# Taking the reciprocal deviation out of the up projection's operand

## What is computed

```python
mod = (silu(c) @ w_ada + b_ada)            # sh1, sc1, g1, sh2, sc2, g2
x = layer_norm(ALPHA * x + g1 * (merged @ w_o), ln1_g, ln1_b)
h2 = x * (1 + sc2) + sh2
up, gt = split(h2 @ w_up, 2)
f = (silu(gt) * up) @ w_down
x = layer_norm(ALPHA * x + g2 * f, ln2_g, ln2_b)
```

## Time and profile before

| what | value |
|---|---|
| median of 3 runs | 526.11 us (525.12 to 526.12) |
| the profiled execution's own time | 526.49 us |
| its span | 524.9 us |
| TensorE busy | 505.6 us, 96% of the span |
| VectorE busy | 294.0 us, 56% |
| ScalarE busy | 223.4 us, 43% |
| GpSimd busy | 90.6 us, 17% |
| mean granted TensorE clock | 0.99 of full speed |

### The profile page before, as it was taken

The page is one execution under the profiler, slowest core; times in us unless marked ns, Lnnn a source line. Parts: engine busy times, 40 slices in busy tenths (PEclk is TensorE's granted clock), DMA queues, the critical chain, the costliest instruction groups (busy, mean ns, idle before and its releaser), DMA issues.

```text
span 524.9 us, 10079 instructions
## 1 busy us (share of the span) xinstructions
PE 505.6 (96%) x3932; PEld 462.0 (88%) x3932; DVE 294.0 (56%) x568; ACT 223.4 (43%) x370; POOL 90.6 (17%) x133
## 2 busy tenths in 40 slices
PE   5899999999999999998999799998999999999997
PEld 3678879888778998997998499998999999999996
DVE  0556676858445453446975966543644445466344
ACT  1434533325435553447436454563444444333312
POOL 2000211126900000000350509631011100000000
PEclk9899999999999999989999999999999999999999
DMA  8999997495996820842654716599777754354102
GB/s 258 394 393 392 381 393 263 143 379 195 326 333 195 272 82 11 253 145 80 240 183 141 240 58 188 165 372 321 277 259 259 261 164 168 136 210 161 41 0 91
DMA packets 85437, 115.80 MB, mean 221 GB/s; under 512 B 3785, under 2 KB 67465, under 8 KB 84884
## 3 DMA queue, kind: packets, MB, share of 16 engines
q1 hardware_dynamic: 83572, 102.76, 58.0%
q0 software_dynamic: 1824, 12.47, 6.4%
HBM read 111.94 MB, written 13.57 MB: 239 GB/s over the span
## 4 chain that ended last, share of the span: by engine, by line
PE 81%; DMA 9%; SPq 3%; DVE 3%; ACT 2%; issue 1%; POOL 0%; DVEq 0%; POOLq 0%; ACTq 0%
PE psum L750 22%; PE psum L752 21%; PE psum L751 21%; DMA raw<-in_w_in 4%; DMA ada_s<-in_w_ada 2%; PE psum L923 2%; PE psum L1043 2%; DMA x_tok<-in_x_sample 2%; PE psum L996 1%; PE psum L1029 1%; PE psum L987 1%; PE psum L782 1%; PE psum L1227 1%; DMA k_early<-in_cache_kv_b 1%; PE psum L771 1%
## 5 line engine op out<-in xcount | busy, mean ns | idle before, releaser
L750 PE MATMUL psum<-act_hi,w_hi 128*128 128x288 f32 x736 | 222.9, 303 | 6.6 <-DVE act_lo L1873 3.3
L499 DVE TENSOR_TENSOR w_lo<-raw,w_hi 128x1024 fp32r<-128x1024 f32 (+1 forms) x120 | 146.0, 1220 | 148.1 <-ACT w_hi L494 147.9
L751 PE MATMUL psum<-act_lo,w_hi 128*128 128x288 f32 x736 | 218.4, 297 | 0.0
L752 PE MATMUL psum<-act_hi,w_lo 128*128 128x288 f32 x736 | 218.0, 296 | 0.0
L494 ACT ACTIVATE w_hi<-raw 128x1024 fp32r<-128x1024 f32 (+1 forms) x120 | 124.1, 1040 | 101.4 <-PE psum L752 81.6
L750 PEld LDWEIGHTS psum<-act_hi,w_hi 128*128 128x128 f32 x736 | 139.4, 189 | 19.7 <-issue 12.5
L752 PEld LDWEIGHTS psum<-act_hi,w_lo 128*128 128x128 f32 x736 | 139.8, 190 | 0.0
L751 PEld LDWEIGHTS psum<-act_lo,w_hi 128*128 128x128 f32 x736 | 139.6, 190 | 0.1
L750 PE MATMUL psum<-f_hi,w_hi 128*128 128x288 f32 x176 | 52.3, 297 | 0.0
L751 PE MATMUL psum<-f_lo,w_hi 128*128 128x288 f32 x176 | 51.9, 295 | 0.0
L752 PE MATMUL psum<-f_hi,w_lo 128*128 128x288 f32 x176 | 51.8, 294 | 0.0
(11 more groups left out here) (214 smaller groups left out, 588.1 us busy)
## 6 DMA issues: line engine op xcount, KB each, us to landing
ada_s<-in_w_ada SPq DMA_DIRECT2D x22, 1024.0 KB, 10.2
raw<-in_w_up SPq DMA_DIRECT2D x22, 1024.0 KB, 5.4
raw<-in_w_in SPq DMA_DIRECT2D x17, 1024.0 KB, 9.8
raw<-in_w_down SPq DMA_DIRECT2D x10, 1024.0 KB, 5.1
out<-in_cache_kv_a POOLq DMA_DIRECT2D x16, 504.0 KB, 6.8
raw<-in_w_o SPq DMA_DIRECT2D x4, 1024.0 KB, 5.8
raw<-in_w_in SPq DMA_DIRECT2D x4, 768.0 KB, 11.0
kvin<-in_cache_kv_a SPq DMA_DIRECT2D x8, 256.0 KB, 3.5
```

Source lines behind the costliest of these rows:

```text
L499: nc.vector.tensor_tensor(part(w_lo, slot4, by_rows), raw_half(rslot, hh, by_rows), part(w_hi, slot4, by_rows).bitcast(F32), ALU.subtract) ...
L750: nc.tensor.matmul(out, hi_l, hi_r, start=start, stop=False, skip_group_check=True)
L751: nc.tensor.matmul(out, hi_l, lo_r, start=False, stop=False, skip_group_check=True)
L752: return nc.tensor.matmul(out, lo_l, hi_r, start=False, stop=stop, skip_group_check=True)
```

## The change

The operand of the up projection becomes h2 * std = (x - mean) * scale + bias * std. The factor 1/std is applied after the matmuls: to each gate unit ahead of the silu, and to each silu ahead of the product. The reciprocal, still in place in `rstd`, moves behind the last `h2_rest`.

- ScalarE scales tiles by the channel scale into `h2_t`: tiles 0 to 3, not yet centred, behind the square of tile 6 and ahead of the next `w_hi`. Tiles 4 to 7, centred by GpSimd, follow between its `act_hi` instructions. `act_hi` becomes a plain copy.
- VectorE makes for tiles 0 to 3 mean * scale - `h2_t` (`minus_centred`), and for every tile std * bias -/+ `h2_t` (`h2_shifted`). `centre_pair` is gone.
- GpSimd makes the sample tokens from `xT`, std and the conditioning, and centres `xT` tiles 0 to 3 too.
- TensorE transposes the two conditioning rows ahead of tile 5 of the first three units.
- In all 11 pairs VectorE has four instructions more, two `gate_t` and two scalings of `silu_t`. TensorE's waits on `silu_ready` become waits on `gate_scaled`.

```diff
         ada_ring(pe, ADA2 + 1)
-        ada_turn(pe, 10)
-        ada_turn(pe, 11)
...
             for k in range(KT):
+                if k == 5:
+                    ada_turn(pe, 10)
+                    ada_turn(pe, 11)
...
                 elif q < 2:
                     pe.wait_ge(f_ready, j * 2 + (q - 1))
                 else:
-                    pe.wait_ge(silu_ready, j * 2 + (q - 1))
+                    pe.wait_ge(gate_scaled, j * 2 + (q - 1))
...
+            if m == 6:
+                for k in range(4):
+                    nc.scalar.activation(h2_t[:, k, 0:PROMPT], xT[:, k, 0:PROMPT], ACT.Copy, scale=mod[:, 32 + k, 0:1]).then_inc(weighted, 1)
             if 4 <= m < 7:
                 hi_static(act, H_UP + m - 4)
...
         h2_leading(1)
+        h2_weighted(4)
         h2_leading(2)
+        h2_weighted(5)
         h2_sample_leading(2, 2, KT)
-        for m in range(3, KT):
+        h2_leading(3)
+        h2_weighted(6)
+        h2_weighted(7)
+        for m in range(4, KT):
             h2_leading(m)
...
                 if q < 2:
-                    act.wait_ge(half_used, nb + 1)
+                    act.wait_ge(gate_scaled, j * 2 + (q + 1))
...
-                    nc.scalar.activation(silu_t[:, q, :], psum[:, q, 0:TOK], ACT.Silu).then_inc(silu_ready, 1)
+                    nc.scalar.activation(silu_t[:, q, :], gate_t[:, q, :], ACT.Silu).then_inc(silu_ready, 1)
...
         dve.wait_ge(off_ready, 2)
-        centre_pair(0)
+        minus_centred(0)
+        minus_centred(1)
         dve.wait_ge(std_ready, 1)
-        V.reciprocal(rstd[:], rstd[:]).then_inc(rstd_ready, 1)
...
+        h2_shifted(0)
+        h2_shifted(1)
         h2_rest(0)
         h2_sample_rest(2, 0, 2)
         h2_rest(1)
-        centre_pair(2)
-        dve.wait_ge(dve_link.sem, dve_link.n)
-        h2_scaled(2)
-        h2_scaled(3)
+        minus_centred(2)
+        minus_centred(3)
+        h2_shifted(2)
+        h2_shifted(3)
         h2_rest(2)
         h2_sample_rest(5, 2, KT)
...
+                if q < 2:
+                    dve.wait_ge(half_used, nb + 1)
+                    if not isinstance(j, int) or j >= 1:
+                        dve.wait_ge(silu_ready, j * 2 + (q - 1))
+                    V.tensor_tensor(gate_t[:, q, :], psum[:, q, 0:TOK], rstd[:], ALU.mult).then_inc(gate_scaled, 1)
                 if q >= 2:
+                    dve.wait_ge(silu_ready, fi + 1)
+                    V.tensor_tensor(silu_t[:, q - 2, :], silu_t[:, q - 2, :], rstd[:], ALU.mult).then_inc(silu_scaled, 1)
+                    dve.wait_ge(silu_scaled, fi + 1)
...
+        pool.wait_ge(centred_s, 1)
+        h2_sample(0, 2)
         centre(4)
-        pool.wait_ge(centred_s, 1)
-        pool.wait_ge(rstd_ready, 1)
-        h2_sample(0, 2)
         h2_sample(2, KT)
         centre(6)
-        pool.wait_ge(centred, 2)
+        pool.wait_ge(weighted, 4)
+        pool.wait_ge(less_mean, 4)
+        centre(0)
+        centre(2)
```

More of the change, by code:

```diff
@@ L361, in build @@
     part_sum, _ = sb("part_sum", [128, 2, TOK], F32, o_tmp + 7 * TOK * 4)
-    off_mean, _ = sb("off_mean", [128, TOK], F32, o_tmp + TOK * 4)
+    off_mean, _ = sb("off_mean", [128, TOK], F32, o_tmp + 11 * TOK * 4)
+    bias_s, _ = sb("bias_s", [128, KT, SAMPLE], F32, o_tmp + 12 * TOK * 4)
+    gate_t, _ = sb("gate_t", [128, 2, TOK], F32, o_tmp + 9 * TOK * 4)
+    assert 12 * TOK + KT * SAMPLE <= 3840
     off_sq, _ = sb("off_sq", [128, TOK], F32, o_tmp + 2 * TOK * 4)
@@ L415, in build @@
         "sums_done", "off_ready", "var_ready", "std_ready", "rstd_ready"))
-    centred = sem("centred")
+    centred, less_mean, weighted = sem("centred"), sem("less_mean"), sem("weighted")
+    gate_scaled, silu_scaled = sem("gate_scaled"), sem("silu_scaled")
     quarters_done, quarters_x, quarters_sq = sem("quarters_done"), sem("quarters_x"), sem("quarters_sq")
@@ L1477, in h2_leading, with h2_weighted @@
             act.wait_ge(h2_ready, m + 1)
-            nc.scalar.activation(act_hi[:, m, 0:PROMPT], h2_t[:, m, 0:PROMPT], ACT.Identity,
-                                 bias=mod[:, 24 + m, 0:1]).then_inc(h2_hi, 1)
+            nc.scalar.activation(act_hi[:, m, 0:PROMPT], h2_t[:, m, 0:PROMPT], ACT.Copy).then_inc(h2_hi, 1)
+        def h2_weighted(m):
+            act.wait_ge(centred, m // 2 - 1)
+            nc.scalar.activation(h2_t[:, m, 0:PROMPT], xT[:, m, 0:PROMPT], ACT.Copy, scale=mod[:, 32 + m, 0:1]).then_inc(weighted, 1)
         def h2_sample_leading(part_n, k0, k1):
@@ L1877, in h2_rest @@
             dve.wait_ge(h2_hi, H2_HI_AT[m])
-            V.scalar_tensor_tensor(act_lo[:, m, 0:PROMPT], h2_t[:, m, 0:PROMPT], mod[:, 24 + m, 0:1], act_hi[:, m, 0:PROMPT].bitcast(F32),
-                                   ALU.add, ALU.subtract).then_inc(h2_lo, 1)
-        h2_scaled(0)
-        h2_scaled(1)
+            V.tensor_tensor(act_lo[:, m, 0:PROMPT], h2_t[:, m, 0:PROMPT], act_hi[:, m, 0:PROMPT].bitcast(F32),
+                            ALU.subtract).then_inc(h2_lo, 1)
+        h2_shifted(0)
+        h2_shifted(1)
         h2_rest(0)
@@ L1892, in _ @@
         for m in range(4, KT):
-            if m in (4, 6):
-                dve.wait_ge(centred, m // 2 - 1)
-            h2_scaled(m)
+            h2_shifted(m)
             h2_rest(m - 1)
         h2_rest(KT - 1)
+        dve.wait_ge(h2_ready, KT)
+        dve.wait_ge(h2s_ready, 2)
+        V.reciprocal(rstd[:], rstd[:]).then_inc(rstd_ready, 1)
         ada_add(10)
@@ L2059, in h2_sample @@
             by_batch = lambda i: mod[:, 8 * i + k0:8 * i + k1, 1:9].unsqueeze(3).broadcast_to([128, nk, DEC_B, DEC_T])
-            step(nc.gpsimd.tensor_tensor(hs, xT[:, k0:k1, PROMPT:TOK], by_token, ALU.mult))
-            step(nc.gpsimd.tensor_tensor(hs4, hs4, by_batch(4), ALU.mult))
-            nc.gpsimd.tensor_tensor(hs4, hs4, by_batch(3), ALU.add).then_inc(h2s_ready, 1)
+            bs = bias_s[:, k0:k1, :]
+            xs4 = xT[:, k0:k1, PROMPT:TOK].rearrange("p k (b t) -> p k b t", t=DEC_T)
+            nc.gpsimd.tensor_tensor(hs4, xs4, by_batch(4), ALU.mult).then_inc(pool_step, 1)
+            pool.wait_ge(std_ready, 1)
+            nc.gpsimd.tensor_tensor(bs.rearrange("p k (b t) -> p k b t", t=DEC_T),
+                                    by_token.rearrange("p k (b t) -> p k b t", t=DEC_T), by_batch(3), ALU.mult).then_inc(pool_step, 1)
+            steps.n = steps.n + 2
+            pool.wait_ge(pool_step, steps.n)
+            nc.gpsimd.tensor_tensor(hs, hs, bs, ALU.add).then_inc(h2s_ready, 1)
+        pool.wait_ge(centred_s, 1)
+        h2_sample(0, 2)
         centre(4)
-        pool.wait_ge(centred_s, 1)
-        pool.wait_ge(rstd_ready, 1)
-        h2_sample(0, 2)
         h2_sample(2, KT)
         centre(6)
-        pool.wait_ge(centred, 2)
+        pool.wait_ge(weighted, 4)
+        pool.wait_ge(less_mean, 4)
+        centre(0)
+        centre(2)
+        pool.wait_ge(centred, 4)
+        pool.wait_ge(rstd_ready, 1)
         pool.wait_ge(h2_lo, KT + 2)
```

23 lines of the change are left out of this document (13 added, 10 removed).

## The result

The changed kernel takes 539.46 us (median of 4 runs, 535.24 to 541.43) against 525.83 (525.12 to 526.12) in the same comparison. The two medians are 13.6 us apart, 2.6%. The ratio estimated over the runs is 1.022, 95% interval [1.017, 1.0274], so slower is clear, and that it is over 2% is not. Slower was forecast, but by 5.5 us, and 539.46 is outside the range. The profiled execution took 538.55 us, its span is 536.9 (12.0 more), the mean granted clock 0.98.

What follows compares the result with a forecast made beforehand. TensorE, busy 505.6 of 524.9 us, was taken as the bound. Terms 1.6 + 0.9 + 0 + 3.0 + 0 = +5.5 gave 532.0 profiled, 531.6 us as median; range 526.0 to 536.0, the forecast's own 529.5 to 534.

Steps and rivals of the forecast that it cites:

- Step 7: Late w_up load near 365: loads and cache copies shift together, 0; bounds -1.5 and +1.5.
- Rival D: Slower by more: clock falls already in the conditioning matmuls or twice (+1.75), late load grows (+1.5): 534.9; 8%.
- Step 5: Clock at the gap before tile 2: falls as before at the same 1.75, so 0; bounds -1.75 and +1.75.
- Step 3: Third operand tile starts +1.6 later, with three GpSimd centrings holding VectorE up by 2.6; contains steps 1 and 2.
- Step 1: Layer norm statistics come +1.2 later, as four ScalarE weightings stand ahead of the next w_hi.
- step 2: First operand tile starts +0.2 later, at about 295.2; ScalarE's second row copy is what is late.
- step 4: Transposes moved ahead of tile 5 lose their cover in TensorE's gap: +0.9, between 0.7 and 1.4.
- step 6: First two pairs of the up projection queue behind VectorE and stall TensorE: +3.0, bounds 1.15 and 4.

Runs made afterwards that it cites:

- e8: Changed kernel with weightings behind the partial sums, GpSimd's centrings of tiles 0 to 3 after the last act_lo, first pair's gate scalings first, copies later and spaced: 524.44 us.
- e11: e8 with both transposes back ahead of the first tile and GpSimd's scalings of xT after the second pair's products: 523.31 us.
- e5: Changed kernel without GpSimd's copies of the sample caches to the outputs: 531.97 us.
- e6: Kernel before the change, without GpSimd's copies of the sample caches to the outputs: 525.09 us.
- e12: Kernel before the change, with GpSimd's burst of nine cache copies begun later and the later copies moved by two units: 529.88 us.
- e2: Changed kernel with the old pairs, so the factor 1/std is left out of gate and silu: 530.87 us.
- e7: Changed kernel with both gate scalings of the first pair ahead of the first w_lo on VectorE: 534.5 us.
- e1: Kernel before the change, with the change's pairs alone and the old layer norm: 533.65 us.
- e4: Changed kernel with GpSimd's centring of tiles 0 to 3 moved behind its wait for VectorE's last act_lo of the samples: 534.14 us.
- e3: Changed kernel with ScalarE's four weightings of tiles 0 to 3 moved behind the copy of the partial sums: 535.69 us.
- e10: Changed kernel with only the cache copies begun later and spaced at 4 units, all outputs written: 531.5 us.
- e9: Kernel before the change, with only the cache copies begun later and spaced at 4 units: 524.64 us.

## Why the prediction was wrong

The 12.0 us between the two profiled executions split as below. The first two rows are read from the two traces. The other four rest on the kernels named in the last column. The 13.6 us between the medians can't be split in this way.

| step | predicted | measured | from |
|---|---|---|---|
| ahead of the change | 0 | +0.30 | square of tile 6, 282.79 against 282.49 |
| 1 to 3, third tile | +1.6 | +2.07 | 301.75 - 282.79 = 18.96 against 16.89 |
| 4, transposes | +0.9 | +0.86 | third tile to first gate, 7.60 in e8, 6.74 in e11 (304.32 - 297.58) |
| 5, clock | 0 | +1.18 | third tile to first gate, 10.23 - 7.60 after, 8.19 - 6.74 before |
| 6, first pairs | +3.0 | +3.07 | B of e5 less B of e6, 218.60 - 215.53 |
| 7, late load | 0 | +4.52 | B less that of the kernel without copies, 6.32 after, 1.80 before |

**Step 7 failed**, the one I gave a sentence: put at 0, it measured +4.52. "Loads and cache copies all hang on the same chain and shift with it": the fifth load shifted by 7.5 us (339.8 to 347.3), the burst only by 5.15. GpSimd's own chain starts 7.7 later (the scalings of `xT`, 321.56 against 313.83), but it has a wait in it that isn't on TensorE's: GpSimd waited 4.40 us for `gain_raw` before, and 2.09 after. Why that wait got shorter no run shows. The runs fall in line by how far behind the burst's start the load that TensorE waits for is issued, and in e12 only the burst was moved:

| kernel | load issued behind the burst's start, us | load takes, us | TensorE idles, us |
|---|---|---|---|
| e2 (new stage, old pairs) | 6.8 | 16.7 | 0.85 |
| before | 6.7 | 17.4 | 1.53 |
| e7 | 2.2 | 19.0 | 2.16 |
| e1 (old stage, new pairs) | 2.2 | 19.9 | 3.10 |
| e4 | 2.2 | 20.2 | 3.37 |
| e3 | 1.6 | 20.3 | 3.50 |
| e12 (before, burst later) | 2.2 | 19.7 | 3.78 |
| after | 2.2 | 20.7 | 3.89 |

With the new layer norm stage alone (e2) loads and burst do shift together, by 3.1 and 3.0 us, as step 7 had it. It is the new pairs that bring them closer. Why TensorE's idle ranges from 2.16 to 3.89 at nearly one distance stays open. The bound of +1.5 was a guess at how much a stall could grow; no row gave when the loads are issued and how long each took. Rival D held this mechanism at 8%, at a third of its size, together with a clock that costs more.

**Step 5** was under-sized by 1.2. I took the old price, since the old clock had fallen too. It now fell before the third tile and stayed low through it. By the runs it isn't a constant: with the new stage A was 21.79, 21.62, 21.60, 20.70 or 19.17 (after, e5, e2, e7, e10), with the old one 19.05 or 17.5. So the +1.18 belongs to this pair of profiled executions; e10 against before gives -1.45 for the same term (308.95 - 301.35 = 7.60, no more than in e8).

**Step 3** was right in kind and short in size: the holds sum to 3.5 us (2.25 - 0.87, 1.89 - 0.87, 1.48 - 0.41), where the walk had 2.6. The third tile came only 0.5 later than forecast, so the walk was long elsewhere. TensorE idled 2.48 ahead of it and not 3.3, since it worked on the two tiles before at the lower clock; in e3, with the clock at 1.00 there, it idled 3.29. The Trainium skill (SBUF — State Buffer, § SBUF: two separate sides) has the lock held for the whole instruction, and by it I had worked out 0.7 more than my walk; the trace, with holds of 1.38, 1.02 and 1.07 us, is nearer to that than to the 0.9 I took from one row. The first hold is nearly the whole centring beside it (1.38, of 1.47), the other two are about three quarters of theirs (of 1.40 each).

**Step 1** (+1.37, predicted 1.2; e3), **step 2** (first tile +0.59, predicted 0.2), **step 4** and **step 6** hold. In step 6 the trace follows the walk: the second gate at t + 3.1 (315.04 - 311.98 = 3.06), the next pair's gate scaled at t + 12.0 (323.85 - 311.98 = 11.87), a stall of 1.6 (1.65), and the third pair's (0.93). These two idles are 2.58 of the 3.07; the other 0.5 isn't placed. The two kernels with spaced copies give the same sum, 218.65 - 215.54 = 3.11.

What stays open: why four runs of the changed kernel spread over 6 us. Their clocks (0.977 to 0.987) spread with them, and only one of the four has a profile.

## What to carry to other kernels

A transfer that is late already is not a constant: before shifting anything ahead of it, list when each load and each burst beside it is issued, and what each waits for, and price what happens if they move by different amounts. A burst of stores that nobody waits for is best spaced out, one group to a stretch of compute; here one changed wait took about 2 us off the old kernel (e9). And when an engine's queue gets a cheap instruction, put it ahead of the waits for another engine, not between them.

## What the runs showed of the hardware

**A load beside a burst.** 1 MB of `w_up` lands in 4.9 to 6.7 us without copies (e5), and in 20.7 beside nine copies. GpSimd had issued the last of the nine by 349.6; the engines were still moving them from 350 to 355. The DMA view for 350 to 355 us of the changed kernel, by queue: packets, MB, share of the 16 engines' time.

```profile
q0 software_dynamic: 118, 1.45, 86.9%
q1 hardware_dynamic: 62, 0.06, 11.1%
```

GpSimd's copies go through q0 in packets of 12 KB, SyncE's load through q1 in packets of 1 KB. The engines were 98% busy, and the load got 4% of the bytes. The Trainium skill (DMA: Bandwidth & Descriptors, § Queues, rings and completion order) says that each DMA engine takes turns between its queues packet by packet. This trace agrees in kind: with such turns a queue of long packets leaves little to one of short packets. It doesn't show turns of one to one (118 packets against 62), so the turns themselves are an explanation and not shown.

**The clock falls with a late load too.** Where TensorE idled 3.89 or 3.78 us in mid-stream, the mean granted clock of 360 to 380 us is 0.83 (changed kernel, e12). Where it idled 3.50, 3.37, 3.10 or 2.16 (e3, e4, e1, e7) it is 0.91; where 1.53 or 0.85 (before, e2), 1.00. The stall of 3.89 thus costs 6.3 in all (B of the changed kernel less that of e5).

**Turns on VectorE.** GpSimd's centrings and VectorE's instructions alternate: each of the three centrings delays one VectorE instruction by 1.0 to 1.4 us. The two that e4 moves behind the critical `act_lo` no longer delay any on the way to the third tile.
